# Products of g times x, with the tokens' inverse roots applied to the results; x loaded in 96-row tiles, zeros written one by one

## The chip, the cores and the metric

The kernel runs on one core of one Trainium2 chip. The metric is device time in microseconds (us). Before the change the median of three runs is 1320.0 us, from 1319.45 to 1322.24.

## The reference

One layer of a hybrid encoder for 256 prompt tokens and 32 sample tokens (288 columns in all), with 2048 features, in float32:

```python
parts = jnp.split(rms_norm(x, g_mix) @ w_in, SPLIT_POINTS, axis=-1)
# stick-breaking q, k, v (8 heads), window q, k, v (8 / 2 / 2 heads), two gates of 2048
q_sw, k_sw = rope(q_sw, pos), rope(k_sw, pos)
o_sb, o_sw = stick-breaking attention, window attention with sinks
g_sb, g_sw = jnp.split(jax.nn.sigmoid(gate_pre + b_gate), 2, axis=-1)
x = x + (g_sb * (o_sb @ w_sb_o) + g_sw * (o_sw @ w_swa_o)) @ w_out
x = x + hier_moe(rms_norm(x, g_ffn), ...)      # 16 experts, 2 for each token
y = rms_norm(x, g_final)
```

`rms_norm(x, g)` is `x * rsqrt(mean(x * x) + 1e-6) * g`, with one inverse root for each token. The new keys and values are outputs too.

## The kernel before, in words

Everything is transposed: features lie on the 128 partitions, the 288 tokens on the free axis. A weight matrix is taken in blocks of 128 output features. Each operand is split in a high half (rounded to float32r) and a low half (the rest), and a block is 16 slices of the contraction times three products, high-high, high-low and low-high, so 48 products of 128x128 by 128x288 (`products`, lines 809 to 822). There are 68 blocks of `w_in` (8 Q and 16 K and V of the stick-breaking part, 8 Q and 4 small K and V of the window part, 16 gates, 16 more gates in the output stage), 16 of the two output projections and 16 of `w_out`. Then 16 experts follow.

The five queues are written out by hand and meet in semaphores. For each block:

- SP loads two blocks of weights (2 MB) at a time into one of two halves of `ring` (line 367), when the low halves of the blocks before are made (`slot_free`).
- ScalarE (`step`, lines 609 to 618) waits for the end of block j (`blk`), copies its result from the bank to its place (`evac`, which raises `ev_a`), then rounds the weights of block j + 2 into `wh` (`split`, line 585).
- VectorE makes the low half `wl` of block j + 2 from `ring` and `wh` (`split`, line 1146).
- TensorE needs `wl` of its block and, by `ev_a`, that the result of block j - 2 has left its bank.

The start: SP loads x in two transfers (lines 362 and 363), the prompt in tiles of 128 rows and the sample in one of 32. ScalarE's queue loads the gains and biases and one table `con` (identity, masks, ones, rotary tables; line 573). SP's first weight loads wait for that table (line 373). TensorE transposes the gains (line 789), then x (line 795), in three banks that VectorE empties into `xT` (line 1123). ScalarE takes the sums of squares (line 579); VectorE works out the inverse roots (lines 1109 to 1118) and three diagonal tiles (line 1131); TensorE spreads them over the partitions by products with ones (line 800), and turns the cached keys (line 806), which ScalarE copies to `kcT_sb` (line 599). VectorE then makes the normalised slices `hbuf` (line 1140), ScalarE rounds each to `xh` (line 593), VectorE takes the rest `xl` (line 1154), and block 0 follows slice by slice.

POOL issues the small loads (lines 461 to 481), after the spill of `xT` two more, sets a zero tile and writes the zeros of the experts' spare rows, 4.5 MB, in one go (line 492). In the K and V loop it copies each head to its place (lines 511 and 515) and stores each group of four (`nat_store`).

In the output stage (lines 712 to 725 and 1295 to 1312) each of 8 passes has two gate blocks and two blocks of output projections. For each m of two, ScalarE makes `sg1` and `sg2` by sigmoids (lines 719 and 720), VectorE merges them with the projections (lines 1304 to 1308) into `m1`, ScalarE rounds it to `mh` (line 724) and then splits weights, VectorE makes `ml` and `wl`.

Of the kernel before, what the change touches and what calls it, by code (L numbers as in the profile page):

```python
# [39 lines left out]
P = 128  # L40
D = 2048
# [118 lines left out]
def build(nc, x_prompt, x_sample, cache_sb_k, cache_sb_v, cache_swa_k, cache_swa_v, w_in, b_gate, swa_sink,  # L160
# [12 lines left out]
    wh = at("wh", 32, [P, 2, KT, P], F32R)  # L173
    wl = at("wl", 48, [P, 2, KT, P], F32R)
# [40 lines left out]
    rstd_b = at("rstd_b", 114, [P, NT])  # L215

    con = at("con", 192, [P, NC_])
    hbuf = at("hbuf", 201, [P, 2, NT])
# [74 lines left out]
    with ExitStack() as ctx:  # L293
        ps = [ctx.enter_context(nc.psum_tensor(f"bank{i}", [P, 512], F32)) for i in range(8)]
        names = """const_in x_in w_load0 w_load1 kc_in vc_in swc_in small_in xT_out act_own dve_own
                   rms diag_done rb_ps x_turned h_done xh_done xl_done xT_done par_ps par_sb kc_ps kc_sb pads
# [64 lines left out]
        def _(sp):  # L361
            sp.dma_start(x_nat[:, 0:2, :], x_prompt[0].rearrange("(t p) d -> p t d", p=P)).then_inc(S["x_in"], 16)
            sp.dma_start(x_nat[0:DEC, 2, :], x_sample[0]).then_inc(S["x_in"], 16)
# [9 lines left out]
            sp.wait_ge(S["const_in"], 16 * 4)  # L373
# [84 lines left out]
        def _(pool):  # L458
            for name in RAISED:
                pool.sem_inc(S[name], 1)  # L460
            pool.dma_start(kc_nat[:], cache_sb_k[0, 0].rearrange("s h d -> s (h d)")).then_inc(S["kc_in"], 16)
# [27 lines left out]
            for r0, k in ((NE * SLOTS, 4), (NE * SLOTS + 4 * P, 0)):  # L489
                n, m = (P, k) if k else (MAXOV * SLOTS - 4 * P, 1)  # L490
                for q in range(m):
                    pool.dma_start(y_rows[r0 + q * P:r0 + q * P + n, :].rearrange("p (b n) -> p b n", n=512),
                                   zero[0:n, :].rearrange("p (a n) -> p a n", a=1).to_broadcast([n, 4, 512]))\
                        .then_inc(S["zero_out"], 16)
# [10 lines left out]
            for n in range(2):  # L505
                with pool.Fori(0, 2) as ii:
                    i = ii + 2 * n
                    for j in range(4):
# [4 lines left out]
                        else:  # L513
# [5 lines left out]
                              sb_kv_sample[ds(i, 1)].rearrange("a p n -> p (a n)"))  # L519
            pool.wait_ge(S["rope_done"], 11)  # L520
# [48 lines left out]
        def _(act):  # L569
# [3 lines left out]
            act.dma_start(con[:], const).then_inc(S["const_in"], 16)  # L573

            act.wait_ge(S["dve_own"], 2)
            act.wait_ge(S["x_in"], 32)
            for t, n in enumerate(TILES):
                own.wait()
                own(a_.activation(squares[0:n], x_nat[0:n, t, :], ACT.Square, accum_out=stat[0:n, t:t + 1]))
# [11 lines left out]
            for k in range(KT):  # L591
                act.wait_ge(S["h_done"], k + 1)
                a_.activation(xh[:, k, :], hbuf[:, k % 2, :], ACT.Copy).then_inc(S["xh_done"], 1)
                if k == 5:
                    split(1, 16)
# [500 lines left out]
        def _(dve):  # L1096
# [55 lines left out]
            for k in range(KT):  # L1152
# [6 lines left out]
                if k == 9:  # L1159
                    split(1, 2)  # L1160
# [421 lines left out]
```

## Time and profile before

| | |
|---|---|
| median of three runs | 1320.0 us |
| the profiled execution | 1323.27 us |
| its span | 1321.6 us |
| mean granted TensorE clock | 0.957 of full speed |
| TensorE busy | 1212.4 us |
| VectorE busy | 465.6 us |
| ScalarE busy | 381.6 us |
| moved by DMA | 340.48 MB |

PE is TensorE's products, PEld its weight loads, DVE VectorE, ACT ScalarE, POOL GpSimd, SP the queue that issues most transfers. "idle ... <- X" says how long an engine stood still before an instruction and what released it. PEclk is the clock that the throttle granted: 1.00 is 2.4 GHz, 0.50 is 1.2 GHz. L819 is line 819 of the kernel before.

### The profile page before, as it was taken

To read this page: it belongs to the slowest core of one execution; us is meant where nothing else is said; L and a number is where in the kernel's file an instruction comes from. 1 tells how busy PE (TensorE), PEld (TensorE's weight loads), DVE (VectorE), ACT (ScalarE), POOL (GpSimd) and SP (SyncE) were. 2 spreads that over 40 slices of the span, in tenths; PEclk is the share of its full clock that TensorE was granted. 3 is DMA by queue.
4 is the path that set the end of the run, shared out by engine and by line. 5 is a ranking of instruction groups with operands and counts; after the bars stand their busy time and mean duration, and the time that the engine had idled before them with its cause. 6 is when DMAs were issued, how large, how long until landed. Compare 5 with 4: busy or idle time off the path is not lost.

```text
span 1321.6 us, 22773 instructions
## 1 busy us (share of the span) xinstructions
PE 1212.4 (92%) x9452; PEld 952.7 (72%) x9452; DVE 465.6 (35%) x705; ACT 381.6 (29%) x481; POOL 63.0 (5%) x107
## 2 busy tenths in 40 slices
PE   4889999999999999999999959999999999998951
PEld 2789999998999999999999944555444444444420
DVE  2723434664544545454544551011100010000027
ACT  3423333334666744554433440000000000000002
POOL 3000101002211000000000000000000000000010
PEclk9889999998999999999999979999999999999975
DMA  9494454443233455455574438999999999999965
GB/s 268 152 323 140 161 195 161 158 160 103 101 124 127 163 177 176 144 173 186 186 263 150 168 128 328 415 428 425 429 428 428 428 427 427 428 428 428 428 192 147
DMA packets 136015, 340.48 MB, mean 258 GB/s; under 512 B 5024, under 2 KB 107552, under 8 KB 113840
## 3 DMA queue, kind: packets, MB, share of 16 engines
q1 hardware_dynamic: 131648, 319.31, 62.6%
q0 software_dynamic: 3936, 17.23, 4.3%
q10 hardware_dynamic: 400, 3.51, 0.7%
q8 instruction: 22, 0.36, 0.1%
q14 instruction: 9, 0.07, 0.0%
HBM read 319.51 MB, written 20.71 MB: 257 GB/s over the span
## 4 chain that ended last, share of the span: by engine, by line
PE 70%; DMA 19%; DVE 4%; SPq 3%; ACT 2%; issue 1%; POOL 0%; POOLq 0%; ACTq 0%; DVEq 0%
PE bank L819 15%; PE bank L821 15%; PE bank L820 15%; DMA home<-in_w_e_up 15%; PE bank L1041 10%; PE bank L1062 5%; PE bank L1021 3%; SPq L395 3%; DMA ring<-in_w_in 2%; DMA yb<-y_rows,rows 1%; PE bank L1049 1%; PE bank L795 1%; DMA con<-in_const 1%; DVE wl L1146 1%; ACT wh L585 1%
## 5 line engine op out<-in xcount | busy, mean ns | idle before, releaser
L819 PE MATMUL bank<-xh,wh 128*128 128x288 f32 x1088 | 332.4, 306 | 10.0 <-DVE xl L1154 5.9
L820 PE MATMUL bank<-xl,wh 128*128 128x288 f32 x1088 | 324.5, 298 | 0.0
L821 PE MATMUL bank<-xh,wl 128*128 128x288 f32 x1088 | 323.7, 298 | 0.0
L1146 DVE TENSOR_TENSOR wl<-ring,wh 128x2048 fp32r<-128x2048 f32 x100 | 229.2, 2293 | 206.7 <-ACT wh L585 206.6
L1041 PE MATMUL bank<-home,hg 128*64 128x512 f32 x1024 | 228.9, 598 | 21.4 <-DMA home<-in_w_e_up 19.8
L585 ACT ACTIVATE wh<-ring 128x2048 fp32r<-128x2048 f32 x100 | 191.0, 1910 | 140.5 <-PE bank L821 129.3
L819 PEld LDWEIGHTS bank<-xh,wh 128*128 128x128 f32 x1088 | 207.3, 191 | 14.8 <-issue 7.8
L821 PEld LDWEIGHTS bank<-xh,wl 128*128 128x128 f32 x1088 | 208.2, 191 | 0.0
L820 PEld LDWEIGHTS bank<-xl,wh 128*128 128x128 f32 x1088 | 208.0, 191 | 0.3
L1041 PEld LDWEIGHTS bank<-home,hg 128*64 128x64 f32 x1024 | 80.3, 138 | 166.3 <-issue 124.3
L1062 PE MATMUL bank<-home,aT 128*64 128x512 f32 x512 | 127.2, 652 | 0.5 <-ACT aT L762 0.5
L1502 DVE SCALAR_TENSOR_TENSOR g_sb<-bank,stat,g_sb 64x512 f32<-64x512 f32 x16 | 12.0, 752 | 238.2 <-ACT g_sb L759 238.2
L1062 PEld LDWEIGHTS bank<-home,aT 128*64 128x64 f32 x512 | 46.2, 149 | 67.6 <-issue 67.0
L759 ACT ACTIVATE g_sb<-bank,stat 64x512 f32<-64x512 f32 x16 | 10.9, 682 | 245.6 <-PE bank L1041 245.6
L1021 PEld LDWEIGHTS bank<-pick,x 96*128 96x128 bf16 x2304 | 71.0, 99 | 14.9 <-issue 12.2
L819 PE MATMUL bank<-oh,wh 128*128 128x288 f32 x256 | 75.9, 296 | 1.8 <-DVE wl L1146 1.8
L1021 PE MATMUL bank<-pick,x 96*128 96x64 bf16 x2304 | 74.6, 195 | 1.6 <-DVE pick L1420 1.6
L819 PE MATMUL bank<-mh,wh 128*128 128x288 f32 x256 | 76.0, 297 | 0.0
L820 PE MATMUL bank<-ol,wh 128*128 128x288 f32 x256 | 75.5, 295 | 0.0
L820 PE MATMUL bank<-ml,wh 128*128 128x288 f32 x256 | 75.5, 295 | 0.0
L821 PE MATMUL bank<-mh,wl 128*128 128x288 f32 x256 | 75.3, 294 | 0.0
L821 PE MATMUL bank<-oh,wl 128*128 128x288 f32 x256 | 75.3, 294 | 0.0
(290 smaller groups left out, 1069.5 us busy)
## 6 DMA issues: line engine op xcount, KB each, us to landing
ring<-in_w_in SPq DMA_DIRECT2D x34, 2048.0 KB, 8.1
home<-in_w_e_gate SPq DMA_DIRECT2D x64, 1024.0 KB, 22.2
home<-in_w_e_up SPq DMA_DIRECT2D x64, 1024.0 KB, 23.4
home<-in_w_e_down SPq DMA_DIRECT2D x32, 2048.0 KB, 20.2
ring<-in_w_out SPq DMA_DIRECT2D x8, 2048.0 KB, 7.6
ring<-in_w_sb_o SPq DMA_DIRECT2D x8, 1024.0 KB, 5.1
ring<-in_w_swa_o SPq DMA_DIRECT2D x8, 1024.0 KB, 7.3
y_rows<-y_sb SPq DMA_DIRECT2D x32, 256.0 KB, 19.9
```

The costliest lines, as they stand in the source:

```text
L395: sp.dma_start(home[c][:, half * 2048:(half + 1) * 2048].rearrange("p (k n) -> p k n", n=DE), src)\
L585: a_.activation(wh[:, j % 2], raw(j), ACT.Copy).then_inc(S["wh_ready"], 1)
L795: mm = tr(ps[2 + k % 3][:, t * P:t * P + n], x_nat[0:n, t, k * P:(k + 1) * P], ident[0:n, 0:n])
L819: mm_(dst, wh[:, j % 2, k, :], hi[:, k, :], start=(k == k0), stop=False)
L820: mm_(dst, wh[:, j % 2, k, :], lo[:, k, :], start=False, stop=False)
L821: mm = mm_(dst, wl[:, j % 2, k, :], hi[:, k, :], start=False, stop=(k == k1 - 1))
L1021: mm_(ps[k // 8][:, (k % 8) * SLOTS:(k % 8 + 1) * SLOTS], x2[j][0:TR, t, k * P:(k + 1) * P], pick[0:TR, t, :], start=(t == 0 and j == 0), ...
L1041: mm = mm_(ps[2][half * SLOTS:(half + 1) * SLOTS, :], hg[:, k, :], gate_up(half, k), start=(k == 0), stop=(k == KT - 1))
L1049: mm = mm_(ps[4][:, f * SLOTS:(f + 1) * SLOTS], g_sb[:, f:DE:FT], ident[0:SLOTS, 0:SLOTS], start=True, stop=True)
L1062: mm = mm_(ps[6 + q // 2][q % 2 * SLOTS:(q % 2 + 1) * SLOTS, :], aT[:, f, :], down(f, q), start=(f == 0), stop=(f == FT - 1))
L1146: v.tensor_tensor(wl[:, j % 2], raw(j), wh[:, j % 2].bitcast(F32), ALU.subtract)\
L1502: v.scalar_tensor_tensor(out=g_sb[:], in0=ps[2][SLOTS:P, :], scalar=stat[0:SLOTS, 24:25], in1=g_sb[:], op0=ALU.mult, op1=ALU.mult).then_in ...
```

## The change

The products now take g times x, not yet normalised. The inverse root of each token is applied to every result as it leaves its bank, by VectorE (`scaled`), and ScalarE evacuates no block any more. For the heads with rotary positions it is multiplied into the two rotary tables once. The gates' biases move into the sigmoids. x comes in three tiles of 96 rows, in four transfers; the identity and the ones come ahead of the rest of the table, which POOL loads behind the first weights; six banks take the transposes in place of three; ScalarE and VectorE share the copy of x and make `xh` and `xl` straight from the bank. The cached keys are turned behind the fourth block. The zeros are written as one piece of 0.5 MB where all five were, and one piece of 1 MB behind the store of each of the four head groups. The core of the diff:

```diff
 @block.sync
-            sp.dma_start(x_nat[:, 0:2, :], x_prompt[0].rearrange("(t p) d -> p t d", p=P)).then_inc(S["x_in"], 16)
-            sp.dma_start(x_nat[0:DEC, 2, :], x_sample[0]).then_inc(S["x_in"], 16)
+            for t in range(2):
+                sp.dma_start(x_nat[0:TR, t, :], x_prompt[0, third(t), :]).then_inc(S[f"x_in{t}"], 16)
+            sp.dma_start(x_nat[0:SEQ - 2 * TR, 2, :], x_prompt[0, 2 * TR:SEQ, :]).then_inc(S["x_in2"], 16)
+            sp.dma_start(x_nat[SEQ - 2 * TR:TR, 2, :], x_sample[0]).then_inc(S["x_in2"], 16)
...
-            sp.wait_ge(S["const_in"], 16 * 4)
 @block.gpsimd
+            pool.wait_ge(S["w_load0"], 16)
+            for a, b in ((C_ID + P, C_ONE), (C_ONE + P, NC_)):
+                pool.dma_start(con[:, a:b], const[:, a:b]).then_inc(S["table_in"], 16)
...
+            zero_rows(NE * SLOTS + 4 * P, MAXOV * SLOTS - 4 * P)
...
                     nat_store(i, nat[:, 0:2, :],
...
+                    zero_rows(i * P + NE * SLOTS, P)
 @block.scalar
-            act.dma_start(con[:], const).then_inc(S["const_in"], 16)
+            for a in (C_ID, C_ONE):
+                act.dma_start(con[:, a:a + P], const[:, a:a + P]).then_inc(S["const_in"], 16)
...
+            a_.activation(stat[0:1, 28:29], stat[0:1, 26:27], ACT.Sqrt)
+            act.wait_ge(S["par_ps"], 1)
+            a_.activation(par[:], ps[1][:, 0:64], ACT.Copy).then_inc(S["par_sb"], 1)
...
+            squared(0)
...
+            for k in range(KT):
+                act.wait_ge(S["x_turned"], k + 1)
+                if k % 2:
+                    a_.activation(xT[:, k, :], ps[2 + k % 6][:, 0:NT], ACT.Copy).then_inc(S["xT_a"], 1)
+                a_.activation(xh[:, k, :], ps[2 + k % 6][:, 0:NT], ACT.Copy, scale=par[:, 32 + k:33 + k])\
+                    .then_inc(S["xh_done"], 1)
+                if k == 5:
+                    split(0, 16)
+                if k == 12:
+                    split(1, 16)
+            squared(2)
...
             with act.Fori(IT_QSB, IT_KSB) as it:
                 for j in range(4):
-                    step(it, j, lambda: a_.activation(flat(qT[:, ds(it * 4 + j, 1), :]), main(j), ACT.Copy)
-                         .then_inc(S["ev_a"], 1))
...
+                    step(it, j, None)
+            for n in range(2):
+                act.wait_ge(S["kc_ps"], n + 1)
+                a_.activation(kcT_sb[:, 4 * n:4 * n + 4, :], ps[5 + n][:].rearrange("p (h n) -> p h n", h=4), ACT.Copy)\
+                    .then_inc(S["kc_sb"], 1)
...
                     act.wait_ge(S["m_done"], m + 1)
-                    a_.activation(sg1[:], flat(gates[:, ds(m, 1), :]), ACT.Sigmoid).then_inc(S["sig_done"], 1)
-                    a_.activation(sg2[:], main(j), ACT.Sigmoid, bias=par[:, ds(m + KT, 1)]).then_inc(S["ev_a"], 1)
+                    a_.activation(sg1[:], flat(gates[:, ds(m, 1), :]), ACT.Sigmoid, bias=par[:, ds(m, 1)])
+                    act.wait_ge(S["ev_a"], m + (EV_PROJ + 1 + 1))
+                    a_.activation(sg2[:], sg2[:], ACT.Sigmoid, bias=par[:, ds(m + KT, 1)]).then_inc(S["sig_done"], 1)
 @block.tensor
+            for t in range(3):
+                pe.wait_ge(S[f"x_in{t}"], 16 if t < 2 else 32)
             for k in range(KT):
-                if k >= 3:
-                    pe.wait_ge(S["xT_done"], k - 2)
...
+                if k >= 6:
+                    pe.wait_ge(*((S["xl_done"], k - 5) if k % 2 else (S["xT_d"], (k - 6) // 2 + 1)))
+                for t in range(3):
+                    mm = tr(ps[2 + k % 6][:, third(t)], x_nat[0:TR, t, k * P:(k + 1) * P], ident[0:TR, 0:TR])
...
             for j in range(4):
...
                 products(IT_QSB, j, xh, xl, first=(j == 0))
+                if j == 0:
+                    pe.wait_ge(S["diag_done"], 3)
+                    for t in range(3):
+                        mm = mm_(ps[2][:, third(t)], ones[0:TR, :], diag[0:TR, t, 0:TR], start=True, stop=True)
+                    mm.then_inc(S["rb_ps"], 1)
+            pe.wait_ge(S["kc_in"], 16)
+            for n in range(2):
+                for h in range(4):
+                    k0 = (4 * n + h) * P
+                    mm = tr(ps[5 + n][:, h * P:(h + 1) * P], kc_nat[:, k0:k0 + P], ident)
+                mm.then_inc(S["kc_ps"], 1)
             with pe.Fori(IT_QSB + 1, IT_KSB) as it:
...
+            pe.wait_ge(S["kc_sb"], 2)
             with pe.Fori(0, 4) as i:
...
 @block.vector
+            for k in range(KT):
+                bank = ps[2 + k % 6][:, 0:NT]
+                dve.wait_ge(S["xh_done"], k + 1)
+                v.scalar_tensor_tensor(out=xl[:, k, :], in0=bank, scalar=par[:, 32 + k:33 + k],
+                                       in1=xh[:, k, :].bitcast(F32), op0=ALU.mult, op1=ALU.subtract)\
+                    .then_inc(S["xl_done"], 1)
+                if k % 2 == 0:
+                    v.tensor_copy(xT[:, k, :], bank).then_inc(S["xT_d"], 1)
+                if k == 6:
+                    own.wait()
+                    split(0, 1)
+                if k == 13:
+                    split(1, 2)
...
+            def scaled(dst, j):
+
+                v.tensor_tensor(dst, main(j), rstd_b[:], ALU.mult).then_inc(S["ev_a"], 1)
+
+            for j in range(4):
+                dve.wait_ge(S["blk"], upto(IT_QSB, j))
+                scaled(qT[:, j, :], j)
+                split((j + 2) % 4, j + 3)
...
+            dve.wait_ge(S["table_in"], 32)
+            for a in (C_COS, C_SIN):
+                own(v.tensor_tensor(con[:, a:a + NT], con[:, a:a + NT], rstd_b[:], ALU.mult))
...
+                    dve.wait_ge(S["blk"], i * 4 + (4 * IT_KSB + j + 1))
+                    scaled(headT[:, j, 0:NT], j)
...
+                else:
+                    dve.wait_ge(S["blk"], upto(IT_KVSW, j))
+                    scaled(headT[:, j, 0:NT], j)
...
+                    dve.wait_ge(S["blk"], i * 4 + (4 * IT_ATT + 2 * u + 1))
+                    scaled(flat(gates[:, ds(i * 4 + 2 * u, 1), :]), 2 * u)
...
                 for j in range(2):
                     m = i * 2 + j
+                    dve.wait_ge(S["m_done"], m + 1)
+                    scaled(sg2[:], j)
                     dve.wait_ge(S["sig_done"], m + 1)
```

## Rows read from the trace of the kernel before

**Rows 1.** The page, busy time and share of the span.

```profile
PE 1212.4 (92%) x9452; PEld 952.7 (72%) x9452; DVE 465.6 (35%) x705; ACT 381.6 (29%) x481; POOL 63.0 (5%) x107
```

**Rows 2.** Waits of TensorE: us in total, times, longest.

```profile
PE bank L789 <- DMA con<-in_const: 14.8, 1, 14.8
...
PE bank L819 <- DVE wl L1146: 5.5, 2, 3.7
```

**Rows 3.** Timeline of the start: start, duration, engine, line, operation, count.

```profile
15.10 13.83 PE L795 MATMUL bank<-con,x_nat 128*128 128x128 f32 x48
...
31.06 1.79 PE L800 MATMUL bank<-diag,con 128*128 128x128 f32 x6 [2.13 <-DVE diag L1131]
...
37.42 0.44 PE L820 MATMUL bank<-xl,wh 128*128 128x288 f32 x1
...
37.66 0.44 PE L821 MATMUL bank<-xh,wl 128*128 128x288 f32 x1
...
54.90 0.41 ACT L623 ACTIVATE qT<-bank 128x288 f32 x1 [0.33 <-PE bank L821]
...
61.59 0.41 ACT L623 ACTIVATE qT<-bank 128x288 f32 x1 [4.48 <-PE bank L821]
```

**Rows 4.** Timeline of ScalarE from 86 us.

```profile
86.36 1.91 ACT L585 ACTIVATE wh<-ring 128x2048 fp32r<-128x2048 f32 x1 [5.16 <-DMA ring<-in_w_in]
...
99.98 0.41 ACT L623 ACTIVATE qT<-bank 128x288 f32 x1 [9.62 <-PE bank L821]
...
106.38 0.41 ACT L623 ACTIVATE qT<-bank 128x288 f32 x1 [4.19 <-PE bank L821]
```

**Rows 5.** Windows: length, busy us by engine (instructions), PEclk, DMA share, GB/s.

```profile
87.00:89.00 2.00, 0.06 (x1) 0.00 (x0) 0.70 (x1) 2.00 (x3) 0.00 (x0) 1.00 1.07 373
90.00:91.00 1.00, 0.26 (x1) 0.29 (x2) 1.00 (x2) 0.36 (x1) 0.00 (x0) 0.50 0.82 289
91.00:96.00 5.00, 5.00 (x22) 5.00 (x22) 1.79 (x1) 0.00 (x0) 0.00 (x0) 0.50 0.38 112
```

**Rows 6.** Windows of the start, the same columns.

```profile
3.00:9.00 6.00, 0.00 (x0) 0.00 (x0) 0.00 (x0) 0.00 (x0) 6.00 (x12) 1.00 1.01 413
...
41.50:42.00 0.50, 0.50 (x4) 0.44 (x3) 0.46 (x2) 0.50 (x1) 0.00 (x0) 1.00 0.06 16
```

**Rows 7.** Groups by shape, 0 to 60 us: count, busy us, mean ns.

```profile
L1140 DVE SCALAR_TENSOR_TENSOR hbuf<-xT,par,rstd_b 128x288 f32<-128x288 f32 x16 | 8.2, 519 | 0.5
L1123 DVE COPY xT<-bank 128x288 f32<-128x288 f32 x16 | 7.3, 457 | 21.0 <-PE bank L795 21.0
...
L579 ACT ACTIVATE squares<-x_nat 128x2048 f32<-128x2048 f32 x2 | 3.8, 1910 | 0.0
...
L806 PE MATMUL bank<-con,kc_nat 128*128 128x128 f32 x8 | 2.0, 428 | 0.0
```

**Rows 8.** Timelines of VectorE and ScalarE in one output pass.

```profile
498.44 2.29 DVE L1146 TENSOR_TENSOR wl<-ring,wh 128x2048 fp32r<-128x2048 f32 x1 [1.23 <-ACT wh L585]
...
498.64 0.48 ACT L720 ACTIVATE sg<-bank,par 128x288 f32<-128x288 f32 x1
...
501.08 0.46 DVE L1304 TENSOR_TENSOR m<-sg,bank 128x288 f32<-128x288 f32 x1 [0.35 <-PE bank L821]
...
504.82 2.29 DVE L1146 TENSOR_TENSOR wl<-ring,wh 128x2048 fp32r<-128x2048 f32 x1 [1.23 <-ACT wh L585]
...
507.56 1.28 ACT L585 ACT_TABLE_LOAD   x1 [2.77 <-PE bank L821]
```

**Rows 9.** Timeline of ScalarE, the copies of the turned keys.

```profile
52.91 1.06 ACT L599 ACTIVATE kcT_sb<-bank 128x512 f32<-128x512 f32 x2
```

**Rows 10.** DMA issues: count, KB each, median us from issue to landing.

```profile
ring<-in_w_in SPq DMA_DIRECT2D x34, 2048.0 KB, 8.1
...
y_rows<-zero POOLq DMA_DIRECT2D x4, 1024.0 KB, 12.8
```

**Rows 11.** Window near 461 us, the columns of rows 5.

```profile
461.00:462.00 1.00, 0.00 (x0) 0.00 (x0) 1.00 (x1) 1.00 (x1) 0.00 (x0) 1.00 0.73 313
```

More of the change, by code:

```diff
@@ L488, in _, with zero_rows @@
             pool.wait_ge(S["zero_set"], 1)
[L489 to L494, printed above, removed]
+            def zero_rows(at_row, n):
+                pool.dma_start(y_rows[ds(at_row, n), :].rearrange("p (b n) -> p b n", n=512),
+                               zero[0:n, :].rearrange("p (a n) -> p a n", a=1).to_broadcast([n, 4, 512]))\
+                    .then_inc(S["zero_out"], 16)
+            zero_rows(NE * SLOTS + 4 * P, MAXOV * SLOTS - 4 * P)
             def nat_store(i, src, dst_prompt, dst_sample):
@@ L689, in _ @@
                     softmax([(0, P), (P, SWC)], sinks[:, ds(i + GRP * u, 1)], hd + 2)
-                    def gate(j):
-                        return lambda: a_.activation(flat(gates[:, ds(i * 4 + j, 1), :]), main(j), ACT.Identity,
-                                                     bias=par[:, ds(i * 4 + j, 1)]).then_inc(S["ev_a"], 1)
-                    step(i + IT_ATT, 2 * u, gate(2 * u))
+                    step(i + IT_ATT, 2 * u, None)
                     act.wait_ge(S["e_done"], hd + 2)
@@ L699, in _ @@
                     a_.activation(pT[:], ps[5][:, 0:SWC], ACT.Copy).then_inc(S["pT_sb"], 1)
-                    step(i + IT_ATT, 2 * u + 1, gate(2 * u + 1))
+                    step(i + IT_ATT, 2 * u + 1, None)
                     act.wait_ge(S["o_sb"], hd + 2)
@@ L1164, in _ @@
             v.memset(kT_sw[:, :, NT:], 0.0).then_inc(S["pads"], 1)
-            with dve.Fori(IT_QSB, IT_KSB) as it:
+            dve.wait_ge(S["table_in"], 32)
+            for a in (C_COS, C_SIN):
+                own(v.tensor_tensor(con[:, a:a + NT], con[:, a:a + NT], rstd_b[:], ALU.mult))
+            own.wait()
+            with dve.Fori(IT_QSB + 1, IT_KSB) as it:
                 for j in range(4):
+                    dve.wait_ge(S["blk"], upto(it, j))
+                    scaled(flat(qT[:, ds(it * 4 + j, 1), :]), j)
                     split((j + 2) % 4, it * 4 + (j + 3))
@@ L1285, in _ @@
                     v.tensor_tensor(lg[:], zm[:], ps[3][:, 0:SBC], ALU.subtract).then_inc(S["e_done"], 1)
+                    dve.wait_ge(S["blk"], i * 4 + (4 * IT_ATT + 2 * u + 2))
+                    scaled(flat(gates[:, ds(i * 4 + 2 * u + 1, 1), :]), 2 * u + 1)
                     split((2 * u + 3) % 4, i * 4 + (4 * IT_ATT + 2 * u + 4))
```

115 lines of the change are left out of this document (36 added, 79 removed).

## The prediction

> **What bounds the kernel now.** I read the page's busy line first: TensorE is busy for 92% of the span [rows 1], so time can only be won where it stands still or runs at half clock, and any other change counts by what it does to those places. Next came the waits of TensorE [rows 2]: 14.8 us at the start for the constants, and two waits for a low weight half (wl), 5.5 us together, of which one is 3.7 us. Then the timeline of the start [rows 3]: the transposes of x begin at 15.10, the first products run from about 37, the first block of 48 products is read out at 54.90 and the second at 61.59. A block at full clock takes 6.40 us (99.98 to 106.38, [rows 4]), so at 61.6 us two blocks, 12.8 us of work, are done: some 48 us go to the front. The third reading is the stretch around 87 us: ScalarE waits 5.16 us for a weight load [rows 4], TensorE does nothing from 87 to 90.7, the granted clock falls to 0.50 (1.2 GHz, [rows 5]), and the next block ends only at 99.98.
>
> The sum is made against the profiled execution: 1323.3 us, of which the span is 1321.6. That is 3.3 us above the median of 1320.0; I carry the difference over to the median.
>
> **The front.** Removed: VectorE's copy, normalisation and rounding of x one after the other, ahead of the products; the wait of the weight loads for the constants; the 1.09 MB table ahead of everything. Added: ScalarE and VectorE split g times x straight from the transposes, the first two weight splits fall into that loop, and the inverse roots are worked out beside block 0.
> 1. TensorE still waits for the constants and all three x tiles. They are 2.5 MB; at the 413 GB/s of 3 to 9 us [rows 6] they end at 9.1 us, the lower bound. The upper one is today's 14.8 [rows 2]. I take 10.5, near the lower end, since the table and the caches no longer share the engines.
> 2. Transposes: the same 288 columns for each of 16 slices, 13.83 us today [rows 3], so up to 24.3.
> 3. Block 0: today's first products follow each other at 0.24 us (37.42, 37.66; [rows 3]) until about 41.3 (from 41.5 on four fit in 0.5 us, [rows 6]) against 0.133 at full clock (6.40 / 48). I take the same 18 slow products, 4.3 us, and 30 at 0.133, 4.0: block 0 ends at 32.6.
> 4. VectorE beside it: ScalarE copies g and makes a square pass first (1.91, [rows 7]), so the loop begins at about 13.2; 16 x 0.52 (as L1140) and 8 x 0.46 (as L1123) [rows 7] and two wl of 2.29 [rows 8] are 16.7, so the last low half is there at 30, before TensorE comes to it. The chain from the sums of squares to diag, about 2 us, ends near 32, together with block 0.
> 5. The products with ones took 1.8 us [rows 3]; at full clock I take 1.0. Block 1 ends at 32.6 + 1.0 + 6.4 = 40.0 in place of 61.5: **-21.5**. Bounds: -23 with the constants at 9.1, -17 with them at 14.8; -18 if block 0 stays at 0.24 throughout (11.5 in place of 8.3).
>
> The x load is now four transfers of 0.25 to 0.77 MB; the row of 3 to 9 us shows 413 GB/s with several transfers open [rows 6]. The Trainium skill, page "DMA: Bandwidth & Descriptors", section "Anatomy of one DMA — SWDGE (gpsimd) path", fits 2.0 us plus bytes over 436 GB/s to one transfer, measured on the GpSimd path. Were that fixed part paid four times in a row, x would be there at about 14 us and the total 3.5 us higher, an estimate from that page; the row speaks for overlap.
>
> **The cached keys.** Eight transposes move from the idle front into the stream, behind block 3. They took 2.0 us at the low clock [rows 7]; at full clock half: **+1.0** (bounds 0.9 and 2.0). Their evacuation to kcT_sb moves too, and brings a wait: TensorE now waits for kc_sb of 2 before the first K block, and ScalarE makes these copies only after its step for the last Q block, that is after that block's end and the weight split of 1.91 us behind it [rows 4], then 1.06 us for the two [rows 9]. TensorE stands for 3.0 us, and every further product is queued behind the wait. The clock fell in the pause at 87, which is about as long [rows 5], so I let it fall here and the next block pays what that one paid: 99.98 less 90.7 is 9.3, less 6.4 is 2.9. **+6.0** (bounds 3.0 without the fall, 6.6 as the whole of the pause at 87).
>
> **The zeros.** Today 4.5 MB go out in one burst (the 1 MB pieces took 12.8 us to land) and delay a weight load, which normally takes 8.1 us [rows 10]. A ring half is free three blocks less a split chain ahead of its use, 3 x 6.4 - 4.2 = 15.0 us. One 1 MB piece at a time is 2.5 us at 413 GB/s, so 10.6 of 15.0: hidden. The pause of 3.7 and the 2.9 of low clock go: **-6.6** (bounds 0 and -6.6). The four issues on POOL's queue stand behind its store of a head group; the next K or V copy there is due a block later.
>
> **Scaling on VectorE.** For 42 blocks (8 Q, 16 K and V, 2 small V, 16 gates) ScalarE's evacuation (0.41, [rows 4]) becomes a VectorE product (0.46, as L1304, [rows 8]). It lies beside ScalarE's weight split, so the chain from a block's end to the next wl falls from 4.6 to 4.2 us, against 6.4 of cover: nothing. If the cover were gone, each us over 6.4 would be paid in all 68 w_in blocks. The scaling of the rotary tables and the memsets (about 2 us, once) end near a block's end: nothing. The last small V head is now scaled behind the sample's softmax, +0.46, and the way into the output stage gets shorter by 0.41: 0 together.
>
> **The output gates.** Here the cover is thin. Today, in each of 8 passes, the second gate's sigmoid (498.64) runs while VectorE makes wl (498.44 to 500.73), and the merge starts at the block's end, 501.08; the wl it leads to ends at 507.11, and TensorE needs it at about 507.5, since ScalarE sees that block's end at 507.56 [rows 8]. The change puts VectorE's scaling behind the first wl (500.75 to 501.2) and the sigmoid behind the scaling (0.48 and two hand-overs of 0.1): the merge starts at 501.9, 0.8 late, of which 0.35 is spare. 8 x 0.5 = **+4.0** (bounds 0 and 6.4).
>
> **Moved queues.** SP's weight loads no longer stand behind the constants, so the first lands near 14.5. POOL's 18 small loads stand behind it, some 12 us later than today; their first reader is TensorE after block 3, beyond 50 us. The table is wanted by ScalarE near 32, 15 us after its issue. The spill of xT leaves earlier. All set at nothing.
>
> **Sum:** -21.5 + 1.0 + 6.0 - 6.6 + 4.0 = -17.1; 1323.3 becomes 1306.2, and the median 1320.0 becomes **1303**. What lies behind the output stage shifts with it, since the expert loads are issued by its blocks.
>
> **The rivals.**
> - *The two new waits cost nothing.* TensorE stands neither before the K blocks nor in the gates: 1303 - 10 = 1293. For it: ScalarE is idle for most of each block. Against: both waits are in program order behind work whose length the rows give. Chance 0.12.
> - *The front saves less.* The constants land as late as today, or the low clock holds through blocks 0 and 1: +4 to +9, 1310. For it: today the second half of block 0 runs at 0.24 or slower after short waits. Chance 0.18.
> - *Slower: the pauses in the gates take the clock with them.* Each of the 8 pauses is followed by a block at half clock, 2.9 each: +23, 1326. It decides if more than 5 of the 8 do so (17 / 2.9). Against: a pause of 1.8 us near 461 passed at a granted clock of 1.00 (2.4 GHz) [rows 11]. Chance 0.05. The Trainium skill, page "TensorE: Matmul & The Clock Gate", section "A second HAM failure mode: psum-queue depth-cycling", tells of such a kernel, where micro-idles between groups of products make the clock oscillate; no row here shows that.
> - *The change does not do what it says.* The PE loop waits for all three tiles anyway, and a zero piece may meet a weight load elsewhere, so the pause at 87 comes back at another place, behind a late front: 1310 + 6.6, 1317. Chance 0.04.
>
> **How the numbers follow.** Forecast 0.61, from 1298 to 1308. The range takes in the hidden waits at 1293 and the late front up to 1312; outside lie the slow rival, the failed change and the ends of the two others, under 0.2. A measurement can tell 0.2%, 2.6 us, from no change. Faster by more: 0.61 + 0.12 + 0.18 = 0.91; within: 0.03, most of the failed change; slower: 0.06, the slow rival and the remainder.
>
> **What would show it.** Right: the second block ends near 40 us; one wait of TensorE for ScalarE's kcT_sb of about 3 us with the granted clock at 0.50 behind it; 8 waits of about 0.5 us for wl in the output gates; no wait for a weight load in the K and V blocks. Wrong: a second block later than 45 us, a wait for kcT_sb under 1 us, gate pauses with a clock below 1.00, or wl waits all through the w_in blocks, which would mean that the split chain has outgrown the block.

## The result, and the profile after

The changed kernel took 1312.7 us (median of 21 executions), the kernel before 1322.0 beside it: a ratio of 0.9942, with an interval of 0.9927 to 0.9958. Faster, as forecast, but by some 8 us (9.3 by the medians) where 17 were expected, and 0.7 us above the upper end of the range, 1312. The kernel before was itself 2.0 us slower here than in the three runs that the forecast starts from (1320.0). One execution at 1547.9 us, at a low granted clock from end to end, is left out of the comparison, so the profile below is that of a further run: 1311.5 us, span 1309.5.

Busy time of the changed kernel, which answers to [rows 1], and waits of TensorE, which answer to [rows 2]:

```profile
PE 1197.4 (91%) x9452; PEld 944.8 (72%) x9452; DVE 481.6 (37%) x743; ACT 370.2 (28%) x445; POOL 61.0 (5%) x109
```

```profile
PE bank L1044 <- DMA home<-in_w_e_up: 26.4, 21, 1.5
PE bank L789 <- DMA con<-in_const: 14.5, 1, 14.5
...
PE bank L809 <- DVE wl L1132: 4.4, 8, 1.2
PE bank L809 <- ACT kcT_sb L639: 3.3, 1, 3.3
```

The constants come at 14.5 us, as late as before (14.8). The wait of 3.7 us for a low weight half, at the zeros, is gone. In its place stand the wait for kcT_sb and eight for wl: seven of 0.4 to 0.5 us in the output passes, and the one of 1.2 where these begin (1.8 before). The wait at the end of the eighth pass, 0.5 us, is put down to the scaling of the gate (L1162).

The start on VectorE, to set beside [rows 3]. Line 1126 is the sum of squares of the second x tile and starts when that has landed; line 1139 makes xl; line 1162 scales a finished block:

```profile
10.25 2.29 DVE L1126 SCALAR_TENSOR_TENSOR wl_scratch<-x_nat 96x2048 f32<-96x2048 f32 x1 [9.20 <-DMA x_nat<-in_x_prompt]
...
17.49 0.52 DVE L1139 SCALAR_TENSOR_TENSOR xl<-bank,par,xh 128x288 fp32r<-128x288 f32 x1 [4.94 <-ACT xh L604]
...
32.48 0.51 DVE L1139 SCALAR_TENSOR_TENSOR xl<-bank,par,xh 128x288 fp32r<-128x288 f32 x1
...
42.80 0.46 DVE L1162 TENSOR_TENSOR qT<-bank,rstd_b 128x288 f32<-128x288 f32 x1 [2.74 <-PE bank L811]
...
82.06 0.46 DVE L1162 TENSOR_TENSOR qT<-bank,rstd_b 128x288 f32<-128x288 f32 x1 [2.08 <-PE bank L811]
...
93.49 0.46 DVE L1162 TENSOR_TENSOR headT<-bank,rstd_b 128x288 f32<-128x288 f32 x1 [7.20 <-PE bank L811]
```

The second block ends at 42.80 in place of 61.59: 18.8 us won at the front. But the first K block ends 11.43 us behind the last Q block, not 6.40. Windows there (length, busy us by engine, PEclk, DMA share, GB/s) show why: TensorE stands, and then runs at half clock.

```profile
80.00:85.00 5.00, 2.02 (x16) 1.78 (x14) 1.46 (x2) 2.88 (x3) 0.00 (x0) 1.00 0.18 62
85.50:88.00 2.50, 2.50 (x11) 2.50 (x11) 0.79 (x1) 0.00 (x0) 0.00 (x0) 0.50 0.10 20
```

VectorE in one output pass, to set beside [rows 8], with the scaling of the second gate (482.61) behind the weight half:

```profile
480.40 2.29 DVE L1132 TENSOR_TENSOR wl<-ring,wh 128x2048 fp32r<-128x2048 f32 x1 [1.23 <-ACT wh L597]
482.61 0.45 DVE L1162 TENSOR_TENSOR sg<-bank,rstd_b 128x288 f32<-128x288 f32 x1
483.77 0.46 DVE L1330 TENSOR_TENSOR m<-sg,bank 128x288 f32<-128x288 f32 x1 [0.71 <-ACT sg L720]
...
487.51 2.29 DVE L1132 TENSOR_TENSOR wl<-ring,wh 128x2048 fp32r<-128x2048 f32 x1 [1.23 <-ACT wh L597]
```

From 480.40 to 487.51 are 7.11 us; the kernel before took 6.38 (498.44 to 504.82). So it goes in each of the 8 passes.

The start of each low weight half is a clock for the whole of the first 750 us: there are 100 in either trace, and the difference of the same one in two kernels says how far one is ahead. The last one of the changed kernel:

```profile
733.53 2.29 DVE L1132 TENSOR_TENSOR wl<-ring,wh 128x2048 fp32r<-128x2048 f32 x1 [1.49 <-ACT wh L597]
```

The same one in the kernel before, and its 16 gate activations, one for each expert (least, median and greatest ns, first and last start):

```profile
746.52 2.29 DVE L1146 TENSOR_TENSOR wl<-ring,wh 128x2048 fp32r<-128x2048 f32 x1 [1.50 <-ACT wh L585]
```

```profile
L759 ACT ACTIVATE g_sb<-bank,stat x16: 682/682/682, 808.4 to 1256.3; 64x512 f32<-64x512 f32 x16
```

So 13.0 us are won by the end of w_out. The first expert's gate activation is at 796.5: 11.9. The last is at 1245.1: 11.2. The span ends 12.1 earlier.

### The profile page after: what moved, and what is told of

Its sections match the earlier page's. It is cut to its first block, busy times and chain, and to the rows that moved or that the text cites. A ratio compares the mean times of both kernels' runs of the same rounds, so it can differ in the third digit from the quotient of the medians.

```text
span 1545.9 us, 22810 instructions
## 1 busy us (share of the span) xinstructions
PE 1467.0 (95%) x9452; PEld 1130.4 (73%) x9452; DVE 483.1 (31%) x743; ACT 370.8 (24%) x445; POOL 58.8 (4%) x109
## 4 chain that ended last, share of the span: by engine, by line
PE 93%; DMA 2%; DVE 2%; ACT 1%; issue 1%; POOL 0%; ACTq 0%; POOLq 0%; SPq 0%; DVEq 0%
PE bank L1044 19%; PE bank L809 17%; PE bank L810 17%; PE bank L811 17%; PE bank L1065 11%; PE bank L1024 6%; PE bank L1052 2%; DMA yb<-y_rows,rows 1%; DMA con<-in_const 1%; PE bank L985 1%; PE bank L935 1%; PE bank L1032 0%; PE bank L817 0%; DVE ya L1574 0%; PE bank L980 0%
## 5 line engine op out<-in xcount | busy, mean ns | idle before, releaser
L809 PE MATMUL bank<-xh,wh 128*128 128x288 f32 x1088 | 368.1, 338 | 3.3 <-ACT kcT_sb L639 3.3
L810 PE MATMUL bank<-xl,wh 128*128 128x288 f32 x1088 | 362.3, 333 | 0.0
L811 PE MATMUL bank<-xh,wl 128*128 128x288 f32 x1088 | 362.2, 333 | 0.0
L1044 PE MATMUL bank<-home,hg 128*64 128x512 f32 x1024 | 294.8, 747 | 1.5 <-DVE hg L1455 1.5
L1044 PEld LDWEIGHTS bank<-home,hg 128*64 128x64 f32 x1024 | 101.3, 153 | 190.9 <-issue 190.9
L809 PEld LDWEIGHTS bank<-xh,wh 128*128 128x128 f32 x1088 | 220.4, 203 | 5.3 <-issue 4.8
L810 PEld LDWEIGHTS bank<-xl,wh 128*128 128x128 f32 x1088 | 220.3, 202 | 0.6
L1065 PE MATMUL bank<-home,aT 128*64 128x512 f32 x512 | 167.8, 827 | 0.5 <-ACT aT L762 0.5
L1024 PEld LDWEIGHTS bank<-pick,x 96*128 96x128 bf16 x2304 | 88.0, 108 | 18.8 <-issue 16.1
L1024 PE MATMUL bank<-pick,x 96*128 96x64 bf16 x2304 | 92.6, 211 | 1.6 <-DVE pick L1445 1.6
L759 ACT ACTIVATE g_sb<-bank,stat 64x512 f32<-64x512 f32 x16 | 10.9, 682 | 292.0 <-PE bank L1044 292.0
```

The source lines that it names most:

```text
L809: mm_(dst, wh[:, j % 2, k, :], hi[:, k, :], start=(k == k0), stop=False)
L810: mm_(dst, wh[:, j % 2, k, :], lo[:, k, :], start=False, stop=False)
L811: mm = mm_(dst, wl[:, j % 2, k, :], hi[:, k, :], start=False, stop=(k == k1 - 1))
L1024: mm_(ps[k // 8][:, (k % 8) * SLOTS:(k % 8 + 1) * SLOTS], x2[j][0:TR, t, k * P:(k + 1) * P], pick[0:TR, t, :], start=(t == 0 and j == 0), ...
L1044: mm = mm_(ps[2][half * SLOTS:(half + 1) * SLOTS, :], hg[:, k, :], gate_up(half, k), start=(k == 0), stop=(k == KT - 1))
L1065: mm = mm_(ps[6 + q // 2][q % 2 * SLOTS:(q % 2 + 1) * SLOTS, :], aT[:, f, :], down(f, q), start=(f == 0), stop=(f == FT - 1))
```

## The experiments

Each ran beside the kernel before on the same chip. "Ahead" is the difference of the last wl from that of the changed kernel's first profile, 733.53; the same kernel once more came to 733.18, so 0.4 of it can be chance. The start of the third wl, just behind the front, differs by 0.6 us among the five traces with the changed kernel's own front.

**The changed kernel, twice.** No edit.

> The changed kernel once more, for a profile that can be set against the one of before by stage. The theory of the forecast, with the constants landing at 14.5 us in place of 10.5: the second block ends near 44 us (about -17), one wait of TensorE for kcT_sb of 3.0 to 3.3 us with the granted clock at 0.50 behind it, no pause like that of 87 us, and eight waits of about 0.5 us in the output gates; these add up to about -13. The measured gain is 7.6, so some 5 us should be found elsewhere. Rival one: the clock also falls at a place where the trace of before has it at 1.00 (a stretch with a clock below 0.95 outside the start and the kcT_sb wait). Rival two: the clock is as before and the 5 us are waits of TensorE in the w_in blocks.

> The changed kernel beside the three others, for their comparison, and a second trace of it. By the ledger of blocks it should end about 11 us before the kernel before (fastest runs 1308.5 against 1319.4), with some executions some 12 us longer; if this profile is one of those, the stage that is longer shows where its granted clock was lost.

The first gave the profile above. The front came to -18.8, the wait for kcT_sb to 3.3 us with the low clock behind it, the pause at 87 us is gone, and the waits in the gates are there. Neither rival holds up to w_out: the clock falls there only at the cached keys and at the sample's softmax (280 to 290 us), and at the second it fell before as well; no w_in block waits for its weights. What the ledger (the sum of these steps) lacks lies behind w_out. The second run of the changed kernel took 1312.5 (four executions, 1310.7 to 1315.7; ratio 0.9929, 0.9905 to 0.9952), and its profile, 1315.7, is one of the longer executions: the first expert comes at the same time (796.2), the last at 1247.3, 2.2 us later, and the end another 2.1 later. The section on the prediction takes this up.

**The zeros alone**, in the kernel before:

```
-for r0, k in (...): ... 4 pieces of 1 MB in one burst
+zero_rows(NE * SLOTS + 4 * P, MAXOV * SLOTS - 4 * P)
...
 nat_store(i, ...)
+zero_rows(i * P + NE * SLOTS, P)
```

> The kernel before with only the zeros written one by one, each behind the store of a head group. The theory of the forecast: the pause of 3.7 us at 87 us and the slow block behind it go, -6.6 us, a ratio of 0.995. Rival: the four pieces meet weight loads further on and the pause comes back elsewhere, or the pause had another cause: a ratio of 1.000 (within 0.002).

1313.8 us, ratio 0.9943 (0.9923 to 0.9963): 6.9 us by the medians. ScalarE's evacuations, to set beside [rows 4], now follow each other at 6.40 us across the place of the pause:

```profile
79.33 0.41 ACT L625 ACTIVATE qT<-bank 128x288 f32 x1 [4.19 <-PE bank L823]
...
85.73 0.41 ACT L625 ACTIVATE qT<-bank 128x288 f32 x1 [4.19 <-PE bank L823]
...
92.13 0.41 ACT L625 ACTIVATE qT<-bank 128x288 f32 x1 [4.19 <-PE bank L823]
```

The block that ended at 99.98 ends at 92.13; 1.4 of the 7.8 us were there already at 75 us, by a clock that came back sooner in the front. The pause and its slow block were worth 6.4. It did not come back elsewhere. This one part, alone, gives as much at the median as the whole change. The 1.4 can only be put down to chance, as the code of the front is the same in both.

**The cached keys copied earlier**, in the changed kernel:

```
-with act.Fori(IT_QSB, IT_KSB) as it: ... 4 steps
+with act.Fori(IT_QSB, IT_QSB + 1) as it: ... 4 steps
 for n in range(2): ... kcT_sb copies
+with act.Fori(IT_QSB + 1, IT_KSB) as it: ... 4 steps
```

> The changed kernel with one part altered: ScalarE copies the turned cached keys to kcT_sb right behind its steps of the first four blocks, before its steps of the next four, so that TensorE no longer waits for them ahead of the first K block. Theory (the wait is caused by program order alone, and costs its 3.3 us and a block at a low granted clock behind it, 5.0 us in all): that pause goes, block 8 ends 6.4 us behind block 7, the end comes 5 us earlier than the changed kernel run beside it. Rival: only the 3.3 us come back, the clock falls for another reason; or nothing comes back, since the end is set by the stream of expert weights whatever its start.

1309.3 us, ratio 0.9895 (0.9864 to 0.9926). The copies now lie at 57.9 us; the wait is gone, and VectorE's scalings show the K block 6.40 us behind the last Q block:

```profile
82.54 0.46 DVE L1165 TENSOR_TENSOR qT<-bank,rstd_b 128x288 f32<-128x288 f32 x1 [2.16 <-PE bank L814]
...
88.94 0.46 DVE L1165 TENSOR_TENSOR headT<-bank,rstd_b 128x288 f32<-128x288 f32 x1 [2.16 <-PE bank L814]
```

5.1 us ahead at the last wl. Three of the four executions ran with a lower granted clock (0.943 to 0.949) and took 1309.1 to 1310.1; the fourth, at 0.973, took 1303.5. So the part is worth its 5 us, and executions of the same kernel lie 6 us apart, which is taken up below.

**The second gate scaled earlier**, in the changed kernel:

```
 v.tensor_tensor(m1[:], m1[:], sg2[:], ALU.add).then_inc(S["m_done"], 1)
+if j == 0:
+    dve.wait_ge(S["m_done"], m + 2)
+    scaled(sg2[:], 1)
```

> The changed kernel with one part altered: in an output pass VectorE scales the second gate right behind the first merge, ahead of the low weight half, in place of behind it. Theory (the second sigmoid and merge are late because the scaling stands behind 2.29 us of weight split): the merge starts at the end of its block again, a pass takes 25.65 us as in the kernel before in place of 26.38, 8 x 0.73 = 5.8 us less than the changed kernel, no wait of TensorE for wl there. Rival: the scaling itself now delays the low half of the first gate's merge, and half of it (0.4 per pass, 3 us) stays.

1309.7 us, ratio 0.9893 (0.9838 to 0.9947), the executions at 1301.9, 1303.8, 1315.6 and 1315.9. No wait for wl stays in the passes, and the merge starts 0.34 behind the weight half again:

```profile
479.55 2.29 DVE L1132 TENSOR_TENSOR wl<-ring,wh 128x2048 fp32r<-128x2048 f32 x1 [1.23 <-ACT wh L597]
482.19 0.46 DVE L1331 TENSOR_TENSOR m<-sg,bank 128x288 f32<-128x288 f32 x1 [0.34 <-PE bank L811]
...
485.93 2.29 DVE L1132 TENSOR_TENSOR wl<-ring,wh 128x2048 fp32r<-128x2048 f32 x1 [1.23 <-ACT wh L597]
```

6.38 us from one to the other, as before the change; 5.8 ahead at the last wl, which is 8 x 0.73. The rival falls.

**Weights held until x is there**, in the changed kernel:

```
+sp.wait_ge(S["x_in2"], 32)
 load_pair(0, w_in[0, :, 0:PAIR])
```

> The changed kernel with one wait added: the first weight loads are issued when the last x tile has landed. It tells why x and the two constant tiles land at 14.5 us. Theory one (the 1 KB packets of the weights share the engines with x; 240 GB/s at a full share in place of 413): constants and x are there at about 9.5 to 10.5, the first weights near 18.5 as now, and VectorE's loop ends 2 to 4 us earlier, as ScalarE meets the first weight split before the weights are there. Theory two (x in 96-row tiles and the small constant tiles are themselves slow): constants still at 14 or later, the weights later by 3 to 5 us, the end later by 1 to 4.

1312.4 us, ratio 0.994 (0.9921 to 0.9958). With no weight on the way, issues and landings (KB each, us to landing) and a window (last columns DMA share and GB/s) are:

```profile
x_nat<-in_x_prompt SPq DMA_DIRECT2D x2, 768.0 KB, 7.3
x_nat<-in_x_prompt SPq DMA_DIRECT2D x1, 512.0 KB, 10.9
x_nat<-in_x_sample SPq DMA_DIRECT2D x1, 256.0 KB, 11.5
con<-in_const ACTq DMA_DIRECT2D x2, 64.0 KB, 10.9
```

```profile
4.00:8.00 4.00, 0.00 (x0) 0.00 (x0) 0.00 (x0) 1.19 (x2) 0.00 (x0) 1.00 1.02 248
```

The engines are full at 248 GB/s, as in the changed kernel (250 in the same window, first line), where the kernel before moved 422 (second line):

```profile
4.00:8.00 4.00, 0.00 (x0) 0.00 (x0) 0.00 (x0) 1.31 (x2) 0.00 (x0) 1.00 1.02 250
4.00:8.00 4.00, 0.00 (x0) 0.00 (x0) 0.00 (x0) 0.00 (x0) 4.00 (x9) 1.00 1.01 422
```

TensorE waits for the constants until 14.1. Theory one falls: the weights don't slow x, x is slow by itself. The last wl starts 1.6 us later than in the changed kernel, as theory two has it; the median is the same.

**x in 128-row tiles**, in the changed kernel:

```
-sp.dma_start(x_nat[0:TR, t, :], x_prompt[0, third(t), :])
+sp.dma_start(x_nat[:, t, :], x_prompt[0, t * P:(t + 1) * P, :])
...
-for t in range(3): mm = tr(ps[2 + k % 6][:, third(t)], x_nat[0:TR, t, ...], ident[0:TR, 0:TR])
+for t, n in enumerate(TILES): mm = tr(ps[2 + k % 6][:, t * P:t * P + n], x_nat[0:n, t, ...], ident[0:n, 0:n])
```

> The changed kernel with x loaded in tiles of 128, 128 and 32 rows as before, in three transfers, with the transposes, sums of squares and products with ones cut to match; the weight loads follow at once as in the changed kernel. Theory one (rows on 96 of 128 partitions are what slows x): x's 8 KB packets take about 0.31 us as in the kernel before in place of 0.54, x and the constants are there at 9.5 to 10.5, ScalarE then stops at slice 6 for the first weights (about 17 to 18), and VectorE's loop ends at 30.5 to 31.5 in place of 32.9: 1.5 to 2.5 us off the end. Theory two (several transfers side by side with the small constant packets are what slows it): still 14 us, and the end where it was, or later by the larger transposes.

1307.6 us, ratio 0.9884 (0.9858 to 0.991). The same views:

```profile
x_nat<-in_x_prompt SPq DMA_DIRECT2D x2, 1024.0 KB, 6.4
x_nat<-in_x_sample SPq DMA_DIRECT2D x1, 256.0 KB, 8.3
con<-in_const ACTq DMA_DIRECT2D x2, 64.0 KB, 7.8
```

```profile
4.00:8.00 4.00, 0.00 (x0) 0.00 (x0) 0.00 (x0) 1.36 (x2) 0.00 (x0) 1.00 1.03 419
```

Theory one holds: 419 GB/s with the weights queued right behind, and TensorE's wait for the constants ends at 10.6. The rows and the number of transfers (three for four) changed together; but a single packet of x, one row of 8 KB, took 0.54 us in the changed kernel and with the weights held, and 0.31 here and in the kernel before (medians of 288 packets), and a packet's own time speaks for the rows. The Trainium skill, page "SBUF — State Buffer", section "Door 1: The DMA port swizzle", says that partitions 0 to 63 lie on one half of the 16 ports and 64 to 127 on the other. By that rule two thirds of a 96-row tile go through half of the ports, which makes 0.75 of the full rate, an estimate from that page. The measurement goes the same way and further: 250 / 422 is 0.59.

VectorE's loop ends at 29.8 in place of 33.0, more than expected, as the weights came by 16.8 (ScalarE's first split) and nobody waited. The second block, however, ends at 41.73, only 1.1 earlier, since TensorE has become the limit. Its products in block 0, here and in the changed kernel:

```profile
25.73 0.44 PE L810 MATMUL bank<-xl,wh 128*128 128x288 f32 x1
25.97 0.44 PE L811 MATMUL bank<-xh,wl 128*128 128x288 f32 x1
...
30.53 0.34 PE L809 MATMUL bank<-xh,wh 128*128 128x288 f32 x1
...
30.84 0.29 PE L811 MATMUL bank<-xh,wl 128*128 128x288 f32 x1
30.97 0.29 PE L809 MATMUL bank<-xh,wh 128*128 128x288 f32 x1
```

```profile
27.70 0.59 PE L809 MATMUL bank<-xh,wh 128*128 128x288 f32 x1
...
30.72 0.32 PE L809 MATMUL bank<-xh,wh 128*128 128x288 f32 x1
30.88 0.29 PE L810 MATMUL bank<-xl,wh 128*128 128x288 f32 x1
```

They start 0.24 us apart and go over to 0.133 at 30.5. In the changed kernel products start later, at 27.70, and go over at nearly the same time, 30.7: fewer of them are slow. At the last wl the version is 2.2 ahead; the second 1.1 arises near 290 us, where the clock, fallen at the sample's softmax in both, came back sooner here. The median is 5 us under that of the changed kernel; what exceeds the 2.2 lies behind w_out, where all four executions ran at a mean clock of 0.97.

**The same with later weight splits**, behind slices 10 and 15:

```
-if k == 5: split(0, 16) ... if k == 12: split(1, 16)
+if k == 9: split(0, 16) ... if k == 14: split(1, 16)
```

> The same with the two first weight splits moved from behind slices 6 and 13 to behind slices 10 and 15 on ScalarE, and by as much on VectorE, so that neither engine meets them before the weights are there. If x is there at 10, VectorE's loop ends near 28 to 29 and the second block near 38.5 to 39.5 in place of 42.8: 3.5 to 4.5 us off the end. If the loop is not what sets the second block (the sums of squares, which need the whole loop on ScalarE), only 2 of them.

1309.2 us, ratio 0.9903 (0.9878 to 0.9929). The second block ends at 41.53: 1.3 us, a miss for both expectations. TensorE's slow products set it, as just seen, and the first of them now also waits for the later weight split:

```profile
25.64 0.61 PE L809 MATMUL bank<-xh,wh 128*128 128x288 f32 x1 [1.04 <-DVE wl L1132]
```

**All together, and the two orders alone.** Early copies of the keys and early scaling of the gate, with 128-row tiles and late splits (first) or with the 96-row tiles left (second).

> All together: 128-row tiles with late splits, the cached keys copied early, the second gate scaled ahead of the weight split. If the three parts add up, w_out ends 4.8 + 5.5 + 4 = 14.3 us earlier than in the changed kernel, and the end comes at about 1297 where the granted clock holds in the expert stage (1308.5 to 1311 for the changed kernel), up to 10 us later where it falls for 6.8 us in every expert. Rival: the stream of expert weights starts no earlier and the end stays at 1303 or above.

> The changed kernel with the two orders mended and x left in 96-row tiles: w_out ends 10.3 us earlier than in the changed kernel, the end comes at about 1300 where the clock holds in the expert stage. It tells whether the gain of the two orders adds up, apart from the front.

1298.4 us, ratio 0.9815 (0.9789 to 0.9841), and 1298.2, ratio 0.9815 (0.9788 to 0.9842). The last wl is 11.7 and 11.3 ahead, where 14.3 and 10.3 were expected. The two orders add up (5.1 + 5.8 = 10.9); the front adds next to nothing. The rival of a fixed expert stream falls: the end moved with w_out.

**Products ahead, and the three mended parts.** In the second, early copies, early scaling and 128-row tiles, with the splits where the change has them; in the first, added to that:

```
+pe.wait_ge(S["warm_set"], 1)
+for _ in range(24):
+    mm_(ps[0][:, 0:P], warm[:], warm[:], start=True, stop=True)
 pe.wait_ge(S["const_in"], 16 * 5)
```

> The three mended parts (128-row tiles, cached keys early, second gate ahead of the split) and, added, 24 small products of a tile of zeros on TensorE while it waits for the constants. Theory one (TensorE starts at half its pace after having stood for 10 us, whatever the rows say of the clock there: 20 products of block 0 at 0.24 us, the transposes of 128 rows at 0.7 to 0.85 us a slice): the first products of block 0 now follow each other at 0.133, VectorE's loop sets the front, and the second block ends 2 to 3 us earlier than in the run beside it without the added products. Theory two (the pace of 0.24 comes from the waits for the low halves of x, or from the transfers running at that time): no difference in the second block, or up to 1 us later by the added work.

> The same without the added products: second block at 41.7 us as in the run with 128-row tiles alone, w_out 4.8 + 5.5 + 1.1 = 11.4 us ahead of the changed kernel, the end at about 1297 to 1298. If 128-row tiles add nothing to the two mended orders, 1298 to 1299.

1297.4 us, ratio 0.9815 (0.9801 to 0.9828), with the added products; 1296.8, ratio 0.9811 (0.9796 to 0.9825), without. With the added work the second block ended 0.45 us earlier (2 to 3 were expected), less than the 0.6 by which equal fronts differ. Its windows show what the others leave open:

```profile
4.00:8.00 4.00, 4.00 (x34) 4.00 (x34) 0.00 (x0) 1.49 (x2) 0.00 (x0) 1.00 1.01 411
8.00:10.00 2.00, 0.58 (x6) 0.39 (x4) 0.28 (x1) 0.00 (x0) 0.00 (x0) 1.00 1.05 226
14.00:18.00 4.00, 4.00 (x16) 2.06 (x14) 3.73 (x9) 3.77 (x9) 1.79 (x4) 0.50 1.09 387
30.00:32.00 2.00, 2.00 (x17) 2.00 (x16) 1.54 (x9) 0.92 (x4) 0.00 (x0) 1.00 0.83 235
```

Here, where the clock has changed once already, the transposes are seen at 0.50 (1.2 GHz), and the products go over at 28.8. So the pace of 0.24 is the low level, as theory one has it. The added products did reach a faster pace: 7 instructions in the microsecond from 4, 12 in that from 6. But TensorE stood for 2.6 us from 8.6 until the constants came, the clock fell at 11.8, and it stayed at 0.50 through the transposes. Theory one is right on the cause and wrong on the cure; theory two falls. The version without the added products has the lowest median of the study, 24 us under the kernel before and 16 under the changed one. The tiles matter little in it: with 96 rows 1298.2, and the intervals overlap.

## Why the prediction was wrong

Up to w_out every step of the sum was found in the trace, with one mechanism missed: the load of x in 96 rows. The sum was too good in the front, in the gates and behind w_out, and too bad at the cached keys. In us, by the profiles:

| Step | Forecast | Measured | From |
|---|---|---|---|
| Front, second block's end | -21.5 | -18.8 | 42.80 against 61.59 |
| Cached keys' transposes | +1.0 | +0.9 | blocks 3 and 4, 55.60 and 62.86 |
| Wait for kc_sb | +6.0 | +5.0 | 93.49 less 82.06 less 6.40 |
| Zeros | -6.6 | -6.4 | the zeros alone |
| Output gates | +4.0 | +5.8 | 8 x 0.73 |
| Other | 0 | +0.5 | remainder, nearly all near 290 us |
| To the last wl | -17.1 | -13.0 | 733.53 against 746.52 |
| Behind w_out, one profile each | 0 | +0.9 | span -12.1 |

**The front (1).** The step that failed is the first: "I take 10.5, near the lower end, since the table and the caches no longer share the engines". The row behind it, 413 GB/s [rows 6], was measured on 128-row transfers, and the change loads 96 rows, which came at 250 GB/s; TensorE began at 14.46, near the upper bound. The estimate named beside it from the Trainium skill, page "DMA: Bandwidth & Descriptors", x at about 14 us, came out in its number, but not by its cause: the DMA engines were full (1.02) at the lower rate, so it is the rate that made x late, not a fixed part paid between transfers. The rest of the step was nearly right. With x at 10.6 the run with 128-row tiles has TensorE's first product at 25.3 (forecast 24.3), the end of block 0 at 34.2 (32.6) and the second block at 41.7 (40.0); it has 21 slow products, where 18 were taken. And the landing, 4.0 us late, cost only 1.1 at the second block, where the prediction had put 4.5 between 10.5 and its upper bound: the 128-row transposes and their waits take 1.5 us longer than the 96-row ones (14.7 against 13.2), and block 0 with its 21 slow products 1.0 longer than with 12. When the pace changes is not fixed: at 28.8 to 34.2 us in the traces with the new front, 30.2 to 31.8 among those with the changed kernel's own. Both the forecast's -21.5 and the -18.8 are counted from one profile of the kernel before; from the run with the zeros alone, whose second block ended at 60.13, it would be -17.3.

**The cached keys.** The wait came as described, 3.3 us for a forecast 3.0, with the clock at 0.50 behind it; the slow stretch cost 1.7 and not 2.9. The rival by which the wait costs nothing is out.

**The zeros** held within 0.2.

**The gates.** The merge started 0.73 us later behind the start of the wl ahead of it than before the change (3.37 us against 2.64), close to the 0.8 forecast, but the spare of 0.35 did not reduce it: the pass lost the whole 0.73. The step that failed is "of which 0.35 is spare". In the trace of before the low half ends at 507.11 and the product behind it starts at 507.28, not "at about 507.5", so the spare was 0.17; and the wait shown, 0.44, is not the whole of the gap, for after the change the two products on either side of it start 0.74 apart in place of 0.13:

```profile
489.12 0.29 PE L811 MATMUL bank<-xh,wl 128*128 128x288 f32 x1
489.86 0.40 PE L809 MATMUL bank<-xh,wh 128*128 128x288 f32 x1 [0.44 <-DVE wl L1132]
```

The granted clock stayed at 1.00, so the rival of pauses that take the clock is out here; the pause at the cached keys, of 3.3 us, did take it.

**Scaling on VectorE and the moved queues** were set at nothing. The remainder of 0.5 arises nearly all near 290 us, between the 38th and the 39th wl, where the clock came back 11.6 us behind the 38th and before the change 10.0; no cost of theirs is to be seen.

**Behind w_out.** "What lies behind the output stage shifts with it" is the other step that failed. In the router TensorE stands for 11.0 us in either kernel, the clock falls, and in this profile it came back later (1.1 us). The expert stage then took 0.7 more, and what follows it 0.9 less. The two profiled executions are 11.8 apart and the medians 9.3: 1.3 of the 2.5 is that the profile of before lies above the median of 1322.0, and 1.2 that this one lies below 1312.7. Executions of the changed kernel scatter more widely than those of before (1308.5 to 1324.9, against 1319.5 to 1325.6), and the experts show where. There are 16. While weights lie ready an expert takes 27.4 us; from the time that TensorE has used them up, 30.6, paced by transfers (12.6 MB loaded and 0.5 stored for each in 30.6 us are 428 GB/s, and the DMA engines are full in the windows below, at 1.01). Windows of the stage in the changed kernel, and in the version with the early second gate, in one of its longer executions:

```profile
800.00:1240.00 440.00, 414.46 (x3731) 207.40 (x3730) 47.87 (x116) 24.28 (x44) 0.00 (x0) 0.99 1.01 424
```

```profile
800.00:1240.00 440.00, 440.00 (x3652) 234.74 (x3650) 46.51 (x113) 23.89 (x43) 0.00 (x0) 0.89 1.01 423
```

In the first, TensorE has 26 us to spare, its waits for the loads. In the second the clock falls once in every expert; TensorE is never idle and takes 30.6 to 30.7 us for each expert but the last from the first on. The lead that the loads had is hardly used. From the first to the last gate activation, with the stage's granted clock:

```profile
L759 ACT ACTIVATE g_sb<-bank,stat x16: 682/682/685, 796.5 to 1245.1; 64x512 f32<-64x512 f32 x16
```

```profile
L759 ACT ACTIVATE g_sb<-bank,stat x16: 682/684/684, 790.2 to 1248.7; 64x512 f32<-64x512 f32 x16
```

That is 448.6 us at 0.99 and 458.5 at 0.89; the kernel before has 447.9 at 0.97. Others go the same way: 447.3 and 447.4 at 1.00 (both orders, 128-row tiles), 450.5 and 451.1 at 0.91 (zeros alone, changed kernel again). So the stage loses nothing down to 0.97 and 10 us at 0.89. In the executions without a profile the time goes with the mean clock of the whole: 1308.5 to 1312.8 at 0.95 or more, 1321.4 to 1324.9 at 0.929 to 0.932. Its fastest execution is 10.9 us under the fastest of before in the same comparison (1319.5), which is near the 12.1 of the profiles; the medians are 9.3 apart.

Shown is that the expert stage is longer where its granted clock is lower. That this makes the longest executions of the changed kernel, of which none was profiled, is argued from their mean clock, which is that of the profile with the early second gate (0.930). What lies behind the last gate activation varies too, from 63.1 to 67.1 us over the traces, and was not taken apart. What decides whether the clock falls in an execution stays open. The kernel before, the versions with 128-row tiles or held weights and that with both orders mended showed a mean clock of 0.95 or more in all executions; the changed kernel and the versions with one order mended fell below 0.95 in about half, and the zeros alone in one of four. No run was made to settle this.

Of the rivals, "The front saves less" is nearest: it named the constants as late as today. Its 1310 is what the two profiles give (1322.0 less 12.1), but it put the whole of the shortfall in the front, where only 2.7 us of it lie.

## What to carry to other kernels

A duration or a rate holds for the shape that it was measured on: 413 GB/s of 128-row transfers did not hold for 96 rows. When an evacuation or a scaling is moved to another engine, look at what stands ahead of it in program order there; here two such places, each a few lines of code, held back 11 us, which the forecast had seen and priced at 10. And ask of the last stage what paces it: where transfers and TensorE are nearly in balance, time won ahead may not reach the end where the clock falls.

## What was not expected of the hardware

- x in 96-row tiles kept the DMA engines full at 250 GB/s; in 128-row tiles they moved 419 to 422.
- The windows of the first 30 us show a granted clock of 1.00 while products follow each other at 0.24 us, nearly twice the 0.133 of full clock. With products ahead of the transposes the same stretch is shown at 0.50. Before the first change of the clock in a trace, the pace of the products says more than the column.
- A pause of 3.3 us cost 5.0 with the slow products behind it, while the pauses of 0.4 to 0.5 us in the output passes left the clock at 1.00. A pause of 2.6 us ahead of the transposes was followed by a clock of 0.50 as well.
- In the expert stage, where TensorE has 6% to spare, a mean clock of 0.97 cost nothing and one of 0.89 cost 10 us of 448.
